# Moving half of the SSD output projection from inside the attention heads to behind the last one

## The reference

```python
y_ssd = yg.reshape(bsz, seqlen, SSD_WIDTH).astype(h.dtype) * ssd_norm_w
...
o = diff_attention(q, k, v, lam, rel_bias)
o = o * lax.rsqrt(jnp.mean(o * o, axis=-1, keepdims=True) + EPS)
y_attn = (o.astype(h.dtype) * subln_w * (1.0 - lambda_init)).reshape(bsz, seqlen, DA_WIDTH)

return jnp.concatenate([y_ssd, y_attn], axis=-1) @ w_out
```

## Time and profile before

| what | value |
|---|---|
| median of 3 runs | 2253.67 us (2253.28 to 2255.93) |
| time of the profiled execution | 2256.08 us |
| its span in the profile | 2254.3 us |
| mean granted TensorE clock, as a share of 2.4 GHz | 0.988 |
| PE busy | 2173.8 us, 96% of the span |
| DVE / ACT / POOL busy | 831.9 / 774.4 / 1110.8 us |

### The profile page before, as it was taken

The page is one execution under the profiler, slowest core; times in us unless marked ns, Lnnn a source line. Parts: engine busy times, 40 slices in busy tenths (PEclk is TensorE's granted clock), DMA queues, the critical chain, the costliest instruction groups (busy, mean ns, idle before and its releaser), DMA issues.

```text
span 2254.3 us, 28782 instructions
## 1 busy us (share of the span) xinstructions
PE 2173.8 (96%) x9940; PEld 1770.8 (79%) x9940; DVE 831.9 (37%) x1446; ACT 774.4 (34%) x1170; POOL 1110.8 (49%) x1476
## 2 busy tenths in 40 slices
PE   7999999999999989999999999999999979999988
PEld 5888888878886667876888888888787868888876
DVE  4222211845822546034222222207743364013136
ACT  4222223334424435323322323325543333222223
POOL 4555554753253214833555555454544546545554
PEclk9999999999999989999999999999999999999999
DMA  5332333232132112521323333322222313333331
GB/s 203 109 96 93 103 103 103 84 94 66 48 103 71 57 52 75 160 65 56 93 94 93 98 103 104 95 92 70 75 84 67 98 43 112 103 103 93 100 106 47
DMA packets 58906, 203.41 MB, mean 90 GB/s; under 512 B 6296, under 2 KB 7704, under 8 KB 58824
## 3 DMA queue, kind: packets, MB, share of 16 engines
q1 hardware_dynamic: 53568, 192.96, 27.4%
q10 hardware_dynamic: 5256, 9.30, 1.2%
HBM read 200.12 MB, written 4.74 MB: 91 GB/s over the span
## 4 chain that ended last, share of the span: by engine, by line
PE 90%; DVE 6%; issue 2%; ACT 1%; POOL 1%; DVEq 0%; ACTq 0%; POOLq 0%
PE bank L426 25%; PE bank L428 25%; PE bank L427 25%; PE bank L488 2%; PE bank L490 2%; PE bank L489 2%; PE bank L667 1%; POOL w_lo L391 1%; PE bank L690 1%; DVE gx_lo L1388 1%; DVE pn_t L1880 1%; PE bank L786 1%; PE bank L594 1%; DVE prob L1656 1%; PE bank L603 1%
## 5 line engine op out<-in xcount | busy, mean ns | idle before, releaser
L391 POOL TENSOR_TENSOR w_lo<-w_raw,w_hi 128x256 fp32r<-128x256 f32 x1456 | 1085.5, 778 | 1096.4 <-ACT w_hi L956 1095.6
L426 PE MATMUL bank<-gx_hi,w_hi 128*128 128x512 f32 x1696 | 669.8, 395 | 30.0 <-DVE gx_lo L1388 13.6
L428 PE MATMUL bank<-gx_hi,w_lo 128*128 128x512 f32 x1696 | 663.5, 391 | 0.0
L427 PE MATMUL bank<-gx_lo,w_hi 128*128 128x512 f32 x1696 | 663.1, 391 | 0.0
L956 ACT CAST w_hi<-w_raw 128x1024 fp32r<-128x1024 f32 x364 | 379.3, 1045 | 386.9 <-PE bank L428 340.6
L426 PEld LDWEIGHTS bank<-gx_hi,w_hi 128*128 128x128 f32 x1696 | 320.2, 189 | 106.0 <-issue 19.3
L428 PEld LDWEIGHTS bank<-gx_hi,w_lo 128*128 128x128 f32 x1696 | 320.2, 189 | 67.8
L427 PEld LDWEIGHTS bank<-gx_lo,w_hi 128*128 128x128 f32 x1696 | 320.6, 189 | 65.0
L426 PE MATMUL bank<-ff_hi,w_hi 128*128 128x512 f32 x352 | 136.9, 389 | 0.0
L427 PE MATMUL bank<-ff_lo,w_hi 128*128 128x512 f32 x352 | 136.9, 389 | 0.0
L428 PE MATMUL bank<-ff_hi,w_lo 128*128 128x512 f32 x352 | 136.9, 389 | 0.0
(11 more groups left out here) (325 smaller groups left out, 2699.4 us busy)
## 6 DMA issues: line engine op xcount, KB each, us to landing
w_raw<-wstream SPq DMA_DIRECT2D x364, 512.0 KB, 3.5
bias_spread<-bias_rows ACTq DMA_DIRECT2D x1, 2560.0 KB
x<-xT ACTq DMA_DIRECT2D x2, 1024.0 KB, 10.5
outT<-ple_o SPq DMA_DIRECT2D x8, 256.0 KB, 2.0
square<-bias_spread ACTq DMA_DIRECT2D x4, 256.0 KB, 2.8
rfin_row<-bias_spread ACTq DMA_DIRECT2D x4, 256.0 KB, 2.7
m_T<-memT ACTq DMA_DIRECT2D x1, 1024.0 KB, 5.3
p_T<-pT ACTq DMA_DIRECT2D x1, 512.0 KB, 4.2
```

Source lines behind the costliest of these rows:

```text
L391: ins = nc.gpsimd.tensor_tensor(w_lo[:, s, part], w_raw[:, s, part], w_hi[:, s, part].bitcast(F32), ALU.subtract)
L426: nc.tensor.matmul(dst, hi, rhs[0], start=first, stop=False)
L427: nc.tensor.matmul(dst, hi, rhs[1], start=False, stop=False)
L428: return nc.tensor.matmul(dst, lo, rhs[0], start=False, stop=last)
```

## The change

A table `HALVES` says how many half tiles stand in each slot of each iteration. The halves keep their order. The new places are: iteration 0 as before; one half, in slot 0, in iterations 1 to 6; one in each slot of iteration 7; two in slot 0 and one in slot 1 of iteration 8; one in slot 0 and two at the very end of iteration 9, behind the last `head_stat` and in front of the wait for `o_col`. So six half tiles leave iterations 1 to 6, two of them come to iteration 7 and four more stand behind it. DVE's additions and ACT's rounding of weight units follow the tiles: a tile that ends in slot 0 is added in front of the copies to `w_T`, one that ends in slot 1 after `o_un`. The load of `m_T` moves behind the last tile.

```diff
+        HALVES = {(0, 0): 1, (0, 1): 1, (1, 0): 1, (2, 0): 1, (3, 0): 1, (4, 0): 1, (5, 0): 1, (6, 0): 1,
+                  (7, 0): 1, (7, 1): 1, (8, 0): 2, (8, 1): 1, (9, 0): 1, (9, 1): 2}
+        def halves_at(h, slot):
+            first_ = sum(n for k, n in HALVES.items() if k < (h, slot))
+            return range(first_, first_ + HALVES.get((h, slot), 0))
+        def units_done_in(h, slots=(0, 1)):
+            return [n // 2 for slot in slots for n in halves_at(h, slot) if n % 2 == 1]
...
-                if h < AH - 1:
-                    ssd_half(h, 0)
-                elif h == AH:
-                    ssd_half(AH - 1, 0)
-                    ssd_half(AH - 1, 1)
+                for n in halves_at(h, 0):
+                    ssd_half(n // 2, n % 2)
                 if 0 < h <= AH:
                     turn(h - 1)
                 if h < AH:
                     for n in range(3, 8):
                         score(h, n // 2, n % 2)
-                    if h < AH - 1:
-                        ssd_half(h, 1)
+                if h <= AH:
+                    for n in halves_at(h, 1):
+                        ssd_half(n // 2, n % 2)
                 if 0 < h <= AH:
                     values(h - 1)
                 if h > 1:
                     head_stat(h - 2)
+            for n in halves_at(AH + 1, 1):
+                ssd_half(n // 2, n % 2)
             pe.wait_ge(sem("o_col"), 1)
...
+                for m in [0] * (h == 0) + [u + 1 for u in (units_done_in(h - 1) if h > 0 else []) if u < AH - 1]:
+                    ahead("mix_ssd", 0, 4, m)
                 if h < AH:
-                    ahead("mix_ssd", 0, 4, h)
                     exps(h, 3, 8)
...
-            act.wait_ge(unit_done, UNIT0["mix_attn"])
-            act.dma_start(m_T[:, :, :], memT.rearrange("(m p) s -> p m s", p=P)).then_inc(sem("m_in"), 16)
             act.wait_ge(sem("o_mean"), 1)
             nc.scalar.activation(o_root[:, :], o_root[:, :], ACT.Sqrt)\
               .then_inc(sem("o_rooted"), 1)
+            for m in [u + 1 for h in (AH, AH + 1) for u in units_done_in(h) if u < AH - 1]:
+                ahead("mix_ssd", 0, 4, m)
+            act.wait_ge(unit_done, UNIT0["mix_attn"])
+            act.dma_start(m_T[:, :, :], memT.rearrange("(m p) s -> p m s", p=P)).then_inc(sem("m_in"), 16)
...
                 if h < AH:
                     for n in range(3, 8):
                         biased(h, n)
+                for m in units_done_in(h, (0,)):
+                    add_ssd(m)
```

More of the change, by code:

```diff
@@ L364, in side_before @@
             return same[-1] + 1 if same else 0
+        HALVES = {(0, 0): 1, (0, 1): 1, (1, 0): 1, (2, 0): 1, (3, 0): 1, (4, 0): 1, (5, 0): 1, (6, 0): 1,
+                  (7, 0): 1, (7, 1): 1, (8, 0): 2, (8, 1): 1, (9, 0): 1, (9, 1): 2}
+        assert sum(HALVES.values()) == 16
+        def halves_at(h, slot):
[3 more added lines that the diff above has]
+            return [n // 2 for slot in slots for n in halves_at(h, slot) if n % 2 == 1]
         block = ctx.enter_context(nc.Block())
@@ L1658, in combine, with add_ssd @@
                 ins.then_inc(sem("diffed"), 1)
+            def add_ssd(m):
+                dve.wait_ge(unit_done, UNIT0["mix_ssd"] + m + 1)
+                nc.vector.tensor_tensor(x[:, m, :], bank[1][:, :], x[:, m, :], ALU.add).then_inc(tile_free, 1)
             def biased(h, n):
@@ L1687, in _ @@
                     nc.vector.tensor_copy(o_un[:, h - 1, :], bank[0][:, :]).then_inc(sem("o_copied"), 1)
[L1688 to L1691, removed]
+                for m in units_done_in(h, (1,)):
+                    add_ssd(m)
+            for m in units_done_in(AH + 1, (0,)):
+                add_ssd(m)
             dve.wait_ge(sem("o_stat"), AH)
@@ L1696, in _ @@
             nc.vector.reciprocal(o_rstd[:, :], o_root[:, :]).then_inc(sem("o_col"), 1)
+            for m in units_done_in(AH + 1, (1,)):
+                add_ssd(m)
             for h in range(AH + 1):
```

## The result

The changed kernel takes 2274.92 us, the median of 4 runs (2266.87 to 2276.38), against 2254.36 us for the kernel before (by now the median of 4 runs too): 20.6 us slower by the medians. The estimate of the ratio, 1.008 with a 95% interval of 1.0068 to 1.0092, comes to 18 us (15 to 21). The forecast was slower too, but by 5.3 us, with a range up to 2267 us. The profiled execution is the fastest of the four (2266.87 us, span 2265.1), so a second profile stands under the first experiment.

A forecast was written before the change was run, and what follows sets the result against it. PE's work was taken to bound the kernel outside the attention, leaving idle time and clock to move. Full-clock terms of -2.2 us plus 7.5 us for the clock gave +5.3 us, 2259.0 us, range 2251.5 to 2267.

The forecast's parts named there:

- What bounded the kernel: Outside the attention PE's work sets the time; the change can move only PE's idle time and PE's clock.
- The sum at full clock: All parts of the change without any fall of the clock: -3.7 - 1.2 - 3.3 + 9.1 - 3.1 = -2.2 us.
- Slot 1 of iterations 1 to 6: A half tile leaves each: 0.92 us gained in three iterations, 0.31 in the other three, 3.7 us in sum.
- The start of iterations 2 to 7: The addition no longer stands between `o_un` and the next biases: 6 x 0.2 = 1.2 us gained.
- The 0.2 us: True waiting between the end of PE's slot 0 half tile and the transposes, counted as gained in six iterations.
- Iteration 7: With two half tiles it becomes like iteration 6 before the change: 17.14 - 13.84 = 3.3 us gained.
- The end: From iteration 8 to the first factor row: 23.05 us against 13.95, 9.1 lost, including a new 0.7 us wait.
- The factor rows: Five rows before the first product: 4.3 us at full clock behind two half tiles, against 7.38, 3.1 gained.
- the term for the clock: At the six new gaps ahead of `values`: 3.75 falls of 2.0 us each, 7.5 us lost; bounds 0 and 20.
- The second rival: Falls of 6.8 us or more come in every iteration of the attention: about +13 us, 2267 us; chance 20%.
- The first rival: Gaps of 2 us are short enough, at most one fall: -2.2 to 0, about 2252 us; chance 22%.

The follow-up runs named there:

- the first experiment: The changed kernel run again with no edit, for a second profile: 2275.53 us, ratio 1.0085 to the kernel before.
- e2: Changed kernel plus 8 or 10 idle matmuls behind the last score in each of iterations 1 to 6 (54 in all): 2253.5 us, ratio 0.9987.
- e5: Changed kernel with the additions of tiles 1, 2 and 3 back behind the copy of `o_un` in iterations 2, 4 and 6: 2261.83 us, ratio 1.0029.
- e3: Kernel before with the six slot 1 half tiles of iterations 1 to 6 left out and put nowhere (72 matmuls fewer): 2255.34 us, ratio 1.0006.
- e6: Changed kernel plus only 4 idle matmuls (0.9 us) behind the last score in each of iterations 1 to 6: 2253.2 us, ratio 0.9989.
- e4: Kernel before with only the first half of tile 7 moved, from iteration 8 to slot 0 of iteration 7: 2244.56 us, ratio 0.9953.
- e7: Kernel before plus 12 and 8 matmuls that compute nothing in slots 0 and 1 of iteration 7: 2251.47 us, ratio 0.9981.

## Why the prediction was wrong, step by step

**What bounded the kernel** was read rightly, and so was the direction. The sum at full clock, -2.2 us, can be held against e2, whose clock never fell there: 1.4 us less than the kernel before by the two profiles between the same points. That the medians differ by just 2.2 us is luck, as 0.8 of it lies outside these stages.

- *Slot 1 of iterations 1 to 6*: forecast 0.92 and 0.31 us gained; measured at full clock 0.80 (13.83 to 13.03) and 0.20. The gaps of "1.9" and "2.5" us are 1.86 and 2.46.
- *The start of iterations 2 to 7*: forecast 1.2 us gained in all, measured 0.6, and only in iteration 2. There PE waited for the addition of tile 0 (the row below this list), though its first score came at 737.69; the prediction's "iterations 2 to 5 look the same" passes over it. In the others nothing was gained: the transposes start 3.97 us after the first score with and without the addition (793.74 to 797.71 before; 751.41 to 755.38 after, 1.24 ahead of the scores at 756.62). The 0.2 us was not a wait that the addition caused.
- *Iteration 7*: 13.9 us at full clock, as forecast; in the changed kernel itself 16.8, since the fall of iteration 6 reaches into it.
- *The end*: forecast 23.05 us, measured 22.5, with the new wait of 0.7 us in its place (0.69). No wait for weights came of the later roundings.
- *The factor rows*: forecast 4.3 us, measured 4.38.

```profile
739.23 0.47 PE L426 MATMUL bank<-ys_hi,w_hi 128*128 128x512 f32 x1 [0.62 <-DVE x L1691]
```

**The step that failed is the term for the clock**, "3.75 falls ... 2.0 us each: 7.5 us lost". That the new gaps would bring the clock down was right; the size was not. The two profiles of the changed kernel lose 16.4 and 21.9 us in iterations 1 to 7, more than twice the term, and the second more than its upper bound of 20. Two things were mis-sized.

- *The count*: five and six falls, not 3.75. I took it from four gaps of about 2 us. A fifth was left out, the 2.18 us ahead of 20.90 in the trace of the kernel before, with low clock from 22.21 on, which makes it three falls of five. Four or five gaps are too few to go by.
- *The length*, and this is the larger part: the price of 2.0 us stands for one stretch of 3.41 us, and the short falls did cost about that (1.6 us each in e5, 1.7 in e3). But five of the six falls at gaps of 2.46 us lasted 13.65 us, longer than anything in the kernel before's attention (3.41 and 6.82 us). Taking the short ones at 1.6, the long ones cost 5.7 to 5.8 us each. All five set in 0.7 to 1.1 us before their gap ended; none of the 14 short falls at the gaps of iterations 1 to 6 (two profiles of this kernel, e3 and e5) set in more than 0.55 us before.

I had counted the addition ahead of the copies as a loss of 0.61 us in three iterations. With all gaps at 1.86 us 13 us come back (e5).

The second rival, "the low clock lengthens itself", foresaw falls of 6.8 us and more, and the long ones are that. Its mechanism is not what the traces show. It blamed the transposes and the paced scores of the next iteration, but all five long stretches end before these begin (787.78 against 787.82 for the one shown above). They run through `values`, three scores and a whole half tile, so my argument against the rival, that this half tile would lift the clock, is refuted as well. Nor did a long fall come in every iteration. Its price of +13 us was too small for the measured +20.6. The first rival, that the clock holds, is refuted as a description of this kernel, and its time (about 2252 us) is near what e2 and e6 give once the gaps are closed (2253.5 and 2253.2).

The rule of the Trainium skill (TensorE: Matmul & The Clock Gate, HAM oscillation) puts the danger at longer gaps than these. The runs here disagree: 11 of the 12 gaps of the two profiles of the changed kernel were followed by 1.2 GHz. The section after it on that page of the Trainium skill, on a second HAM failure mode, tells of an engine that idles briefly but often between groups of matmuls, so that its clock swings. The 11 falls agree with it, though its case is another one and no run here tests its cause.

The length of a gap alone does not decide. At one place behind the attention PE has a gap of 2.6 us with dense matmuls on both sides. In the first profile of the changed kernel:

```profile
911.43 0.38 PE L439 MATMUL bank<-m_hi,w_hi 128*128 128x256 f32 x1 [2.56 <-DVE m_lo L1739]
911.43:914.90 3.47, 3.47 (x29) 3.47 (x30) 0.17 (x1) 2.23 (x3) 1.11 (x2) 1.00 0.38 137
```

This gap is longer than the dear ones and no fall followed. Over all ten profiles it is 2.6 to 2.8 us long and was followed by a fall in six of them, never for longer than 3.4 us. So something besides the length counts, in what stands around the gap or in when it comes; which of them was not tested.

What stays open: why falls at gaps of 2.46 us could last four times as long, and why one gap of 1.86 us is followed by a fall and the next is not, in the same kernel with the same instructions. It differs from execution to execution (iteration 3 in the two profiles), so it is not the kernel's order alone. No run tests it.

## What to carry to other kernels

Moving work out of a loop in which PE alternates with DVE leaves a gap in every turn, and its price can be the clock of all the work around it, here more than ten times what the waits themselves changed: 20.6 us lost against 1.4 gained at full clock. Before moving work to where PE waits, count what covers the place it leaves; one half tile in the one uncovered place (e4) gave 11 us, six moved half tiles cost 20. Where a gap can't be closed with useful work, a few matmuls into a bank that is overwritten next can close it enough (e6), and an instruction on another engine that lengthens the gap by 0.6 us can cost far more than 0.6 us (e5).

## What the hardware showed that was not expected

- A low stretch of TensorE's clock can last through 5.3 us of dense matmuls (a whole half tile, 782.56 to 787.82): at five of the six gaps of 2.46 us it ran 13.65 us, across `values`, three scores and a half tile (mean clock 0.51 from 774.0 to 787.8), and ended ahead of the transposes.
- Ahead of `values`, gaps of 0.7 and 1.3 us left no trace in the clock (e6), gaps of 1.86 us were followed by a fall of 3.4 us in 13 of 18 cases (iterations 1 to 6 of both profiles of the changed kernel, e3 and e5), and gaps of 2.46 us in 6 of 6, five of them long. Elsewhere the same lengths do otherwise: 2.6 us between dense matmuls often did nothing, and 1.11, 0.78 and 0.93 us in a row stood in front of 6.8 us of low clock in the kernel before.
- The same kernel varies by 9 us and more (2266.87 to 2276.38), while kernels whose clock holds in the attention vary by 3 to 4 (2251.14 to 2254.5 in e2, 2243.17 to 2247.25 in e4). It is not all a matter of how much low clock there is: e7 varies by 8.5 us (2246.31 to 2254.79) with a mean clock of 0.991 or 0.992 in every run.
